# Channel sums of the first layer, and the sample state update of 32 rows per product, in a 4-layer decoder step

## The reference, cut to what matters

```
def layernorm(x, g, b):
    mu = jnp.mean(xf, axis=-1, keepdims=True)
    var = jnp.mean(jnp.square(xf - mu), axis=-1, keepdims=True)
    return ((xf - mu) * lax.rsqrt(var + EPS)).astype(x.dtype) * g + b

def chunk_mlp(h, ...):                       # layer 0
    u, v = jnp.split(jax.nn.gelu(h @ w_in + b_in), 2, axis=-1)
    v = layernorm(v, ln_g, ln_b)             # over 1024 channels
    ...                                      # mixing of positions with w_s, then (u * mixed) @ w_out

def step(s, xs):                             # layer 3, per head; s is 128 x 128
    v_new = u_c - jnp.einsum('bhck,bhkv->bhcv', w_c, s)
    ...
    s = (s * jnp.exp(g_last)[..., None, None]
         + jnp.einsum('bhck,bhcv->bhkv', k_c * jnp.exp(g_last[..., None] - g_c)[..., None], v_new))
```

## Time and profile before

| | |
|---|---|
| Median of 3 runs | 1576.44 us (1575.49 to 1576.65) |
| The profiled execution | 1579.24 us, its span 1577.5 us |
| Busy: TensorE, its weight load | 1532.6 us (97%), 1491.9 us (95%) |
| Busy: VectorE, ScalarE, GpSimd | 799.8 (51%), 735.9 (47%), 1087.9 us (69%) |
| Granted TensorE clock, mean | 0.991 of full speed |
| Moved by DMA | 212.48 MB, 135 GB/s |
| Ones-products of layer 0, lines 989 and 996 | 8 and 8, in 34 to 67 us |
| Products of the sample state update, lines 1338 and 1339 | 16, in 1170 to 1303 us |

### The profile page before, as it was taken

How to read it: one execution, slowest core, us unless ns; L and a number is a source line. 1 busy time by engine, 2 the same in 40 slices (tenths; PEclk the granted TensorE clock), 3 DMA queues, 4 the chain that set the end, 5 groups by cost and what they waited for, 6 DMA issues and landing times.

```text
span 1577.5 us, 32573 instructions
## 1 busy us (share of the span) xinstructions
PE 1532.6 (97%) x10374; PEld 1491.9 (95%) x10374; DVE 799.8 (51%) x1777; ACT 735.9 (47%) x1406; POOL 1087.9 (69%) x1044
## 2 busy tenths in 40 slices
PE   6999999999999999999999999999899999999997
PEld 5999999998999999887999999999888989999997
DVE  3365555106555412996655521666668766554411
ACT  5555444345444334656544434557534324444332
POOL 5557888774777678985877777666645655777674
PEclk9999999999999999999999999999999999999998
DMA  5434445453444655221565445544312224444453
GB/s 196 133 112 148 146 155 168 132 145 98 160 146 146 164 149 174 91 81 58 168 169 154 142 135 149 185 134 138 132 60 64 68 82 169 160 149 145 126 154 105
DMA packets 87678, 212.48 MB, mean 135 GB/s; under 512 B 25424, under 2 KB 33136, under 8 KB 87472
## 3 DMA queue, kind: packets, MB, share of 16 engines
q1 hardware_dynamic: 87600, 211.49, 43.1%
HBM read 201.80 MB, written 9.66 MB: 134 GB/s over the span
## 4 chain that ended last, share of the span: by engine, by line
PE 92%; DVE 4%; ACT 1%; issue 1%; DMA 1%; POOL 0%; DVEq 0%; SPq 0%; POOLq 0%; ACTq 0%
PE bank L871 26%; PE bank L872 26%; PE bank L873 26%; PE bank L1233 2%; PE bank L1094 2%; PE bank L1255 1%; PE bank L1244 1%; PE bank L1293 1%; PE bank L1147 1%; PE bank L1323 0%; DVE bank L2132 0%; PE bank L1338 0%; DMA fst<-in_d_st 0%; PE bank L1339 0%; DMA raw<-in_a_in 0%
## 5 line engine op out<-in xcount | busy, mean ns | idle before, releaser
L595 POOL TENSOR_TENSOR wlo<-raw,whi 128x512 fp32r<-128x512 f32 (+3 forms) x400 | 461.3, 1153 | 388.4 <-ACT whi L1386 350.7
L871 PE MATMUL bank<-Gh,whi 128*128 128x320 f32 x1928 | 604.5, 314 | 18.8 <-DVE Gl L1871 15.7
L872 PE MATMUL bank<-Gl,whi 128*128 128x320 f32 x1928 | 597.0, 310 | 0.0
L873 PE MATMUL bank<-Gh,wlo 128*128 128x320 f32 x1928 | 597.0, 310 | 0.0
L597 POOL TENSOR_TENSOR wlo<-raw,whi 128x512 fp32r<-128x512 f32 (+2 forms) x400 | 481.9, 1205 | 0.0
L1386 ACT ACTIVATE whi<-raw 128x1024 fp32r<-128x1024 f32 (+3 forms) x400 | 374.8, 954 | 49.3 <-PE bank L873 39.9
L871 PEld LDWEIGHTS bank<-Gh,whi 128*128 128x128 f32 x1928 | 363.0, 188 | 22.6 <-issue 15.4
L872 PEld LDWEIGHTS bank<-Gl,whi 128*128 128x128 f32 x1928 | 363.3, 188 | 1.5
L873 PEld LDWEIGHTS bank<-Gh,wlo 128*128 128x128 f32 x1928 | 363.1, 188 | 0.0
L871 PE MATMUL bank<-Hh,whi 128*128 128x320 f32 x912 | 284.1, 312 | 4.0 <-DVE Hl L2073 2.5
L872 PE MATMUL bank<-Hl,whi 128*128 128x320 f32 x912 | 282.3, 310 | 0.0
(11 more groups left out here) (364 smaller groups left out, 1823.1 us busy)
## 6 DMA issues: line engine op xcount, KB each, us to landing
raw<-in_f_up SPq DMA_DIRECT2D x176, 512.0 KB, 3.5
raw<-in_f_down SPq DMA_DIRECT2D x64, 384.0 KB, 3.1
raw<-in_f_down SPq DMA_DIRECT2D x64, 320.0 KB, 3.1
raw<-in_c_pw SPq DMA_DIRECT2D x24, 512.0 KB, 3.7
raw<-in_a_in SPq DMA_DIRECT2D x16, 512.0 KB, 3.9
raw<-in_d_qk SPq DMA_DIRECT2D x16, 512.0 KB, 3.8
raw<-in_d_vg SPq DMA_DIRECT2D x16, 512.0 KB, 3.6
raw<-in_a_out SPq DMA_DIRECT2D x8, 512.0 KB, 3.5
```

Of the source, the lines that this page charges most:

```text
L595: pool.tensor_tensor(wlo[k][:, 0:half], raw[k][:, 0:half], whi[k][:, 0:half].bitcast(F32), ALU.subtract).then_inc(half_ready, 1)
L871: nc.tensor.matmul(dst, wh, h, start=start and n == 0, stop=False)
L872: nc.tensor.matmul(dst, wh, lo, start=False, stop=False)
L873: ins = nc.tensor.matmul(dst, wl, h, start=False, stop=stop and end and n == len(tiles) - 1)
```

## The change

**Sums of layer 0.** `v_sum(m)` is new on VectorE: after gelu m, for m = 1 to 7, it adds tile m to a running sum that lies in the bank `mixb[0]`; the first add reads tiles 0 and 1, and the last writes `ssq` in SBUF. The adds stand one behind each eviction from the third on, the last ahead of eviction 8. `v_mean()` is now one ones-product of `ssq`, between units 8 and 9, and waits for the seventh add. `v_square_sum(m)`, for m = 1 to 3, adds the first four squares in the same way behind eviction 9. `v_var()` is one product of their sum and one each of squares 4 to 7, all between units 10 and 11. ScalarE's squares 4 to 7 wait for VectorE's adds (`vsq_read`) in place of products, and the root waits for `vvar_done`.

**Sample state update.** The product of columns 0 to 511 reads rows 0 to 31 of `kdec[x]` and `VX[x]`, that of columns 512 to 1023 rows 32 to 63, in place of all 128. `VX` is written as before.

```diff
-            def v_mean(m):
-
-                pe.wait_ge(gelu_done, m + 1)
-                if m == 0:
-                    pe.wait_ge(std_ready, 1)
-                ins = nc.tensor.matmul(stat[:, 0:NT], ones[:, :], tile_of(V3, m), start=m == 0, stop=m == KT - 1)
-                if m == KT - 1:
-                    ins.then_inc(vmean_done, 1)
-
-            def v_var(m):
-
-                pe.wait_ge(vsq_ready, m + 1)
-                nc.tensor.matmul(mixb[2][:, 0:NT], ones[:, :], vsq[m % 4][:, 0:NT], start=m == 0, stop=m == KT - 1)\
-                    .then_inc(vsq_read, 1)
+            def v_mean():
+
+                pe.wait_ge(std_ready, 1)
+                pe.wait_ge(v_sums, KT - 1)
+                nc.tensor.matmul(stat[:, 0:NT], ones[:, :], ssq[:, :], start=True, stop=True).then_inc(vmean_done, 1)
+
+            def v_var():
+
+                pe.wait_ge(vsq_read, 4)
+                nc.tensor.matmul(mixb[2][:, 0:NT], ones[:, :], ssq[:, :], start=True, stop=False)
+                for m in range(4, KT):
+                    pe.wait_ge(vsq_ready, m + 1)
+                    ins = nc.tensor.matmul(mixb[2][:, 0:NT], ones[:, :], vsq[m % 4][:, 0:NT], start=False, stop=m == KT - 1)
+                ins.then_inc(vvar_done, 1)
...
-            for n in range(4, 8):
-                v_mean(n - 4)
+            for n in range(4, 9):
                 in_unit(n, n % 4)
-            v_mean(4)
-            in_unit(8, 0)
-            for m in range(5, KT):
-                v_mean(m)
+            v_mean()
             in_unit(9, 1)
-            for m in range(4):
-                v_var(m)
             in_unit(10, 2)
-            for m in range(4, KT):
-                v_var(m)
+            v_var()
             in_unit(11, 3)
...
-                        nc.tensor.matmul(bank[4 * x][:, :], T(kdec[x], 2), VX[x][:, 0:512], start=True, stop=True)
-                        nc.tensor.matmul(bank[4 * x + 1][:, :], T(kdec[x], 2), VX[x][:, 512:1024], start=True, stop=True)\
-                            .then_inc(sx_done, 1)
+                        nc.tensor.matmul(bank[4 * x][:, :], T(kdec[x], 2)[0:32, :], VX[x][0:32, 0:512], start=True, stop=True)
+                        nc.tensor.matmul(bank[4 * x + 1][:, :], T(kdec[x], 2)[32:64, :], VX[x][32:64, 512:1024],
+                                         start=True, stop=True).then_inc(sx_done, 1)
...
-                    act.wait_ge(vsq_read, KT)
+                    act.wait_ge(vvar_done, 1)
...
-            for n in range(9):
+            def v_sum(m):
+
+                run = mixb[0][:, 0:NT]
+                dve.wait_ge(gelu_done, m + 1)
+                if m > 1:
+                    dve.wait_ge(v_sums, m - 1)
+                vec.tensor_tensor(ssq[:, :] if m == KT - 1 else run, tile_of(V3, 0) if m == 1 else run, tile_of(V3, m),
+                                  ALU.add).then_inc(v_sums, 1)
+
+            def v_square_sum(m):
+
+                run = mixb[0][:, 0:NT]
+                dve.wait_ge(vsq_ready, m + 1)
+                if m > 1:
+                    dve.wait_ge(vsq_read, m)
+                vec.tensor_tensor(ssq[:, :] if m == 3 else run, vsq[0][:, 0:NT] if m == 1 else run, vsq[m][:, 0:NT],
+                                  ALU.add).then_inc(vsq_read, 2 if m == 1 else 1)
+
+            for n in range(8):
                 a_evict(n)
+                if n >= 2:
+                    v_sum(n - 1)
+            v_sum(KT - 1)
+            a_evict(8)
             dve.wait_ge(vmean_done, 1)
             for m in range(KT):
                 v_centre(m)
             a_evict(9)
+            for m in range(1, 4):
+                v_square_sum(m)
             a_evict(10)
```

More of the change, by code:

```diff
@@ L210, in trunk_kernel @@
         vmean_done, vcentred, vsq_ready, vsq_read = sem("vmean_done"), sem("vcentred"), sem("vsq_ready"), sem("vsq_read")
-        vn_done = sem("vn_done")
+        vn_done, v_sums, vvar_done = sem("vn_done"), sem("v_sums"), sem("vvar_done")
         sig_ready, z_ready, ca_done = sem("sig_ready"), sem("z_ready"), sem("ca_done")
```

## The result

The changed kernel takes 1569.72 us (median of five runs, 1569.12 to 1570.65) against 1576.65 us for the kernel before beside it. The ratio is 0.9946, with a 95% interval of 0.9933 to 0.9958: faster by 6.9 us, where 6.4 was forecast. The profiled execution took 1569.98 us, its span 1568.3.

The account below looks back on a forecast made before the run. TensorE was taken to bound the kernel, with 92% of the span on the chain that ended last. Gains of 4.9 + 1.5 = 6.4 us off 1576.44 gave 1570.0 us, own range 1569.0 to 1571.2, whole range 1567.2 to 1574.0.

Parts of the forecast that it names:

- Part 1: Channel sums of layer 0: ten ones-products of 0.537 us go, 5.37 less 0.44 lost, 4.9 us gained.
- What is late next: Layer 0, unit 4: TensorE waits for GpSimd's low parts, ready at 34.31, so 0.44 us of the gain is lost.
- The sentence on adds with two SBUF inputs: Layer 0, VectorE's first adds: even at 1.41 us beside GpSimd, the add ends before the next eviction at 34.1.
- The hand-over to TensorE: Layer 0, unit 4: from GpSimd's finished low parts to TensorE's start, estimated at 0.07 us.
- The adds and their waits: Layer 0, VectorE: ten adds of 0.49 us in idle time, mean add 2 us early, root not later, no cost.
- Part 2: Sample state update at the four pair ends: 0.5 + 0.27 + 0.27 + 0.5 = 1.5 us gained.
- I take 3 passes: A head's two products at a pair end: partly overlapped, three passes, 1.28 us in place of 1.71.
- full overlap: Rival at the pair ends: products wholly side by side, 2 passes, 2.3 us gained there, 1569.2 us in all; chance 0.08.
- The trip: Each pair end: changing the number of rows and going back costs TensorE 0.39 us.
- Head 1 and the borders: Pair ends: head 1 waits for GpSimd's copies; VectorE is late at the middle borders, which give 0.27 us each.
- The clock: Rival, stays at 1.2 GHz, 1.6 us each: two more, 1573.2, chance 0.08; one or two fewer, 1567 to 1568.4, 0.08.

Follow-up runs that it names:

- e2: The kernel before with only the sample state update changed (32 rows per product), layer 0 as before: 1575.07 us, ratio 0.998.
- e4: The kernel before with both sample state products of a head on the same rows 0 to 63: 1581.29 us, ratio 1.0014.
- e5: The kernel before, unchanged, run once more for its profile; no time is given, its trace agrees with the first within 0.03 us up to 369 us.
- e1_sums_only: The changed kernel with the old sample state products on 128 rows, so only layer 0's sums differ from before: 1573.8 us, ratio 0.9965.
- e9: The changed kernel with GpSimd's masked copies cut to 64 rows of 512 columns per head from 128 of 1024: 1566.17 us, ratio 0.9921.

## Why the prediction was right, and where its steps were not

The total is right to 0.5 us, and partly by luck: two terms were off in opposite ways. By the traces the change brings 4.6 + 2.3 = 6.9 us. Two more comparisons of the same two kernels gave 8.0 and 8.2 us, so the measured 6.9 is known to about 1 us.

**Part 1, forecast 4.9, measured 4.6.** The price of a product (0.537) and the count of ten hold: 5.48 us come out once unit 4 doesn't wait. The step that failed is "What is late next", by its size: GpSimd's half was taken as ready at 34.31 as before, and it was ready at 34.53. The first add reads two SBUF tiles, took 1.02 us, and GpSimd's masks beside it took 1.96 in place of 1.70. The sentence on adds with two SBUF inputs asked only whether VectorE is in time, not what its step does to GpSimd, which was the engine that unit 4 waits for. The hand-over to TensorE took 0.15 and not 0.07. So where the sum counts 0.44 of the product as lost, unit 4 is 0.21 later than before, and 0.74 are lost: 5.37 - 0.74 = 4.63. That the adds do this to the masks is shown by their coming and going together: the first mask step takes 1.09 or 1.10 us in the four traces without the adds (`before`, `e2`, `e4`, `e5`) and 1.34 to 1.38 in the seven that have both side by side. The Trainium skill has the rule for it ("SBUF — State Buffer", section "Who interferes with whom": a VectorE step with two SBUF inputs and a GpSimd step that reads SBUF exclude each other for the whole step). The trace agrees on both engines: the add begins while GpSimd works, ends 0.36 us after that GpSimd step, and GpSimd's next step is 0.26 us longer. How long the add lasts hangs on where it meets the other: 1.02 us for the first add here, 0.49 in `e1_sums_only`, 0.57 for the first add of squares.

**The adds and their waits.** As forecast: ten adds, eight of them of 0.49 or 0.50 us, the mean's done 1.7 us ahead of the mean product, units after the fourth without waits, the root not later.

**Part 2, forecast 1.5, measured 2.3.** By pairs 0.86, 0.31 and 0.32, and 0.94 behind the last one, less 0.10 for the entry of the first: 2.3. The second figure is inferred, since in the three traces with the old products that pair had a stay (43.64, less 1.62 = 42.02; `e4`'s pair without a stay, 42.36 less its trip of 0.34, gives the same). The step that failed is "I take 3 passes". It reasoned that the second product must wait until the first has gone through its two passes. The rows show the other bound: both products' first passes together, then both second ones. The rule of the Trainium skill ("TensorE: Matmul & The Clock Gate", Part 3, products on different row groups start almost together) would have given it, as the rival *full overlap*, which had 0.08; the trace agrees, with 0.01 us between starts. This rival's sum, 0.9 + 0.27 + 0.27 + 0.9 = 2.3, is what was measured. With the rule stated for just this arrangement, its chance should have been above that of 3 passes, which no row supported.

**The trip.** 0.39 forecast, 0.34 measured with one group of rows. `e9` shows the same parts of it: a longer first and last slot (0.54 and 0.52 against 0.43) and 0.10 more in the first ones-product. "TensorEngine Tiling (Array Packing)", Key Properties, of the Trainium skill says that such a change drains the engine. The trace agrees in that the first product starts 0.10 us later behind the one ahead of it (1169.77 to 1170.09 in `e4`, 1169.77 to 1169.99 before).

**Head 1 and the borders.** Head 1 waited for GpSimd as forecast, for 0.25 us. VectorE had no idle time before the next pair's first step at the first two borders, and TensorE waited 0.29 us for its state adds at the second. That the middle borders give only what VectorE's slack allows held: 0.27 forecast, 0.31 and 0.32 measured.

**The clock.** It was a rival with two chances. The change neither brought nor took stays as far as these traces tell: some stand in all or most traces, the others come at other places in each execution, 1.0 to 1.7 us each. The single traces differ by 9.2 us in span, the medians by 6.9; the 2.3 between them is stays and no effect of the change.

## What to carry to other kernels

Products whose rows are mostly zero can be put on different row groups and run side by side, if they stand next to each other and everything they read is ready: an interruption between them cost twice its length here. When a step is moved to an idle engine, look at which neighbour shares its port, and what waits for that neighbour. When a product stops reading part of a tile, stop writing that part: here that was worth more again than the packed products (3.1 and 2.3 us).

## What the runs showed of the hardware

- Two float32 products of 512 columns on rows 0 to 31 and 32 to 63 take the time of one: a pair end has four pass slots of 0.43 us in place of eight. Going to fewer rows and back costs 0.34 us in all (`e4`). On the same 64 rows nothing is gained.
- A VectorE add of 320 columns takes 0.49 us with one bank and one SBUF input, and 0.49 to 1.05 us with two SBUF inputs beside GpSimd: it ends 0.35 to 0.38 us after the GpSimd step that it met, and the next GpSimd step, where it follows at once, is 0.24 to 0.28 us longer.
- VectorE's two query steps, with two SBUF inputs each, ended 0.75 us after GpSimd's copies at the first border, whether the copies were long (before, after) or short (`e9`).
- GpSimd's masked copy of 128 x 1024 took 1.90 us, that of 64 x 512 1.03: 46% less for half the rows and half the columns. What the rows alone do was not run.
- Two executions of one kernel agreed within 0.03 us over 369 us, and later differed by steps of about 1.6 us: stays at the lower clock. Three of six stood at the same places in both; ahead of those in the pairs TensorE was busy for 8.5 us or more of 10. Such a step is no effect of an edit unless it stays through several traces.
